# Hybrid decoder block: first norm's scales moved into the token transfer, the first roundings and warm-ups rearranged, the residual transposes moved behind the query tiles

## The chip, the cores and the metric

The kernel runs on one core of one Trainium2 chip. The metric is the device time of one execution in microseconds (us), lower is better. Engines are named as in the profile: PE is TensorE's matmuls and PEld its weight loads, DVE is VectorE, ACT is ScalarE, POOL is GpSimd, SP is SyncE, which here only issues transfers.

## What is computed

One layer of a decoder block on 256 tokens of width 1024, float32. Cut to what matters here:

```python
def reference(x, ...):
    xn = rmsnorm(x, norm1_g)                    # per token: x * rsqrt(mean(x*x) + EPS) * g
    x = x + hybrid_mixer(xn, ...)               # conv branch + dilated attention, both gated, then W_out
    hn = rmsnorm(x, norm2_g)
    return x + peer(hn, ...)                    # product keys: query projection, scores, top 16, experts

def hybrid_mixer(xn, w_in, ...):
    proj = xn @ w_in                            # GLU input, q, k, v, two gates: 5376 columns
    ...
def peer(xn, w_q, sub_keys, u_tab, v_tab):
    q = (xn @ w_q)                              # 8 heads x 2 halves of 128: 16 query tiles
    s = einsum(q, sub_keys)                     # scores against 2 x 128 keys a head
    ...                                         # top 16 of 16 x 16 candidates, softmax -> gate
    h = einsum(u_tab[e], xn)                    # computed densely: all 128 U tiles
    return einsum(gelu(h) * gate, v_tab[e])     # and all 128 V tiles
```

## The kernel before, in words

**Layout.** The tokens lie transposed in `resid`, [128, 8, 256]: feature in the partition, eight blocks `k` of 128 features, 256 tokens as columns. All weights come as tiles of [128, 1024] (512 KB), 76 for the front (`front`: 8 GLU, 12 q and k, 6 v, 16 gates, 6 attention, 4 convolution and 8 mixer output tiles, then 16 query tiles, numbers 60 to 75), then 128 of U and 128 of V. Every tile goes through a ring of four slots: SP loads it into `raw` (L387), ScalarE rounds it to `hi` (`split_hi`, L335), VectorE or GpSimd makes the rest `lo = raw - hi` (`split_lo`, L354), and TensorE forms three products for each block k, hi x high part, hi x low part, lo x high part of the vector: 24 matmuls of 256 columns for one tile (`product`, L1218). `by_dve` says which engine makes a tile's lower half: VectorE for tiles 0 and 1 and for every fourth tile (3, 7, ... 75), GpSimd for the others. `load` of tile n waits for the lower half of tile n - 4, `split_hi` of tile n for TensorE's end of tile n - 4, TensorE's tile n for its lower half. Each engine works its queue in the order in which the code writes it.

**The start.** TensorE first runs `WARM_UP` matmuls on a tile of ones (L1233; two passes each in the profile). SP issues the tokens in two transfers of four blocks (L382, `x_in`), then tiles 0 to 2, the parameters, tile 3. ScalarE issues a transfer of its own for norm 1's scales (L475, `gain_in`). Norm 1 isn't applied before the first GLU tiles: these take `x * g` instead, and the factor of each token is applied to the result. The high part `xg_hi` of the first `XG_ACT` = 5 blocks is made by ScalarE (L481), that of the last three by VectorE (L748); the low part `xg_lo` of all eight by VectorE (`x_lo`, L738). The first two tiles' high products (L1242) run first, then their lower products (L1249), then the same for tile 2, then the sums of squares of the tokens (L1265, `ssq1`), for which ScalarE squares (L485, L488) and VectorE adds in pairs (L756, L760). Then come ScalarE's root (L493), VectorE's reciprocal (L764) and the normalisation for all later tiles.

**The middle.** After the GLU tiles, VectorE runs 31 taps of the depthwise convolution for four blocks (L794, L798) between its other work. Attention, convolution and mixer tiles follow; the mixer's output is added into `resid` (L975).

**The query tiles.** In the loop over u of the 16 query tiles (60 + u), ScalarE casts tile 63 + u and, for u from 4 to 11, the high part of block u - 4 of norm 2 (L469). VectorE makes a lower half where `by_dve` says so, then the normalisation of block u - 4 (`normalise`, L727 and L719), then the scaled copy of the query tile (`times_rs2`, L982). TensorE runs tiles 0 and 1, the sums `ssq2`, then tile 2, and behind tile 2 the 16 transposes of `resid` into banks 0 to 3 (L1440, `y_began`), where the V products add to them at the end. After tile 15 come 64 score matmuls (L1451), whose results ScalarE copies out (L639), and then the loop over the U tiles. GpSimd, when it has made all its lower halves up to tile 78, waits for `y_began`, writes `iota_nk` (L456) over memory that `resid` held, and goes on with the U tiles' lower halves, the next of which waits for ScalarE's cast of tile 79.

Of the kernel before, what the change touches and what calls it, by code (L numbers as in the profile page):

```python
# [11 lines left out]
ALU = mybir.AluOpType  # L12
# [3 lines left out]
P = 128  # L16
D = 1024
T = 256
# [36 lines left out]
WARM_UP = 27  # L55
# [17 lines left out]
XG_ACT = 5  # L73
# [92 lines left out]
def hybrid_block(nc, x_t, front, cols, rel_bias, onehot, sub_keys, u_tiles, v_tiles, out):  # L166
    bias_row = nc.dram_tensor("bias_row", (HEADS, BW), F32, kind="Internal").ap()
    toeplitz = nc.dram_tensor("toeplitz", (HEADS, P * BW), F32, kind="Internal").ap()
    with ExitStack() as ctx:
# [19 lines left out]
        def tmp(name, shape, dt=F32):  # L189
            return sb(name, shape, dt, inner)  # L190
# [28 lines left out]
        resid = tmp("resid", [P, KB, T])  # L219
# [50 lines left out]
        gain_in = sem("gain_in")  # L270
        square_run, acc_pairs = sem("square_run"), sem("acc_pairs")
        hi_ready = sem("hi_ready")
# [107 lines left out]
        def _(sp):  # L380
            for r in range(2):
                sp.dma_start(resid[:, 4 * r:4 * r + 4, :], x_t[:, 4 * r:4 * r + 4, :]).then_inc(x_in[r], 16)  # L382
# [82 lines left out]
        def _(a):  # L465
# [9 lines left out]
            a.dma_start(prm[:, C_N1:C_N1 + KB], cols[:, C_N1:C_N1 + KB]).then_inc(gain_in, 16)  # L475
            a.preload_act_table(ACT.Sqrt)
            a.wait_ge(gain_in, 16)
            for k in range(XG_ACT):
                if k % 4 == 0:
                    a.wait_ge(x_in[k // 4], 16)  # L480
                a.activation(xg_hi[:, k, :], resid[:, k, :], ACT.Copy, scale=prm[:, C_N1 + k:C_N1 + k + 1])\  # L481
                 .then_inc(xhi, 1)
            split_hi(a, 0, 0, 0)
# [218 lines left out]
        def _(dve):  # L702
# [12 lines left out]
            def normalise(gain, round_, ks):  # L715
# [7 lines left out]
                for k in ks:  # L723
                    if round_ == 0:
# [3 lines left out]
                                             scalar=prm[:, gain + k:gain + k + 1],  # L728
# [5 lines left out]
            def x_lo(k):  # L734

                dve.wait_ge(xhi, k + 1)
                i, gain = k % KB, (C_N1, C_N2)[k // KB] + k % KB
                dve.scalar_tensor_tensor(out=xg_lo[:, i, :], in0=resid[:, i, :], scalar=prm[:, gain:gain + 1],  # L738
# [3 lines left out]
            dve.wait_ge(gain_in, 16)  # L742
            for k in range(XG_ACT):
                if k % 4 == 0:
                    dve.wait_ge(x_in[k // 4], 16)
                x_lo(k)
            for k in range(XG_ACT, KB):
                dve.tensor_scalar(xg_hi[:, k, :], resid[:, k, :], prm[:, C_N1 + k:C_N1 + k + 1], None, ALU.mult)\  # L748
                   .then_inc(xhi, 1)
                x_lo(k)  # L750
# [121 lines left out]
            for n in range(T_ATT):  # L872
                if n > 0:
                    lo_of(n + LEAD)
                if n in NORM_AT:
                    normalise(C_N1, 0, NORM_AT[n])
# [108 lines left out]
            for u in range(HALVES):  # L985
# [6 lines left out]
                if 4 <= u < 4 + KB:  # L992
                    normalise(C_N2, 1, (u - 4,))
# [204 lines left out]
        def _(pe):  # L1198
# [37 lines left out]
            def high_products(b, n):  # L1236

                pe.wait_ge(hi_ready, n + 1)
                for k in range(KB):
                    pe.wait_ge(xlo, k + 1)  # L1240
# [192 lines left out]
            for u in range(2, HALVES):  # L1433
                step(full(T_WQ + u, ("wq", u), xg_hi, xg_lo))
                if u == 2:

# [191 lines left out]
```

## Time and profile before

| | us |
|---|---|
| median of 3 runs | 996.57 (996.49 to 997.5) |
| the profiled execution | 997.07 |
| its span in the profile | 995.2 |
| outside the span | 1.87 |
| TensorE busy | 989.8 |
| VectorE busy | 774.9 |
| ScalarE busy | 506.8 |
| GpSimd busy | 465.3 |

Times in the profile count from the start of the span. An engine's busy time is the union of its instructions' times; a matmul row's time runs to its modelled end, which overlaps the next one's start, so how fast products follow each other is read from where rows start, or from the chain of waits, whose pieces join without a gap. The chain goes back from the last instruction, at each step to what released it.

### The profile page before, as it was taken

How to read it: one execution, taken by the hardware profiler on the slowest of the kernel's cores; microseconds unless marked ns; L12 is line 12 of the kernel's file. 1: busy time of each engine (PE TensorE's matmuls, PEld its weight loads, DVE VectorE, ACT ScalarE, POOL GpSimd, SP SyncE). 2: the span in 40 equal slices, each digit the busy share in tenths (PEclk: the TensorE clock that was granted, in tenths of full speed). 3: DMA queues.
4: the chain of work that ended last, by engine and by line, in shares of the span. 5: the costliest groups of instructions: out<-in, count | busy, mean ns of one | idle time of the engine just before them, and what ended most of it. 6: DMA issues, size and time to landing. Idle time of an engine off the chain costs nothing.

```text
span 995.2 us, 21854 instructions
## 1 busy us (share of the span) xinstructions
PE 989.8 (99%) x7822; PEld 917.0 (92%) x7822; DVE 774.9 (78%) x1304; ACT 506.8 (51%) x789; POOL 465.3 (47%) x198
## 2 busy tenths in 40 slices
PE   9999999999999999999999999999999999999998
PEld 9998999999999999999999999888888888888887
DVE  5999784868899996097777777988888876776764
ACT  6663877544555544544444444444444445554443
POOL 3664366656689999874444444100000004344442
PEclk9999999999999999999999999999999999999999
DMA  6684445654455565555555555555554555556562
GB/s 242 211 308 150 149 148 162 212 201 149 150 197 200 171 211 188 191 176 184 177 180 174 182 172 169 185 175 170 177 180 171 182 174 190 190 189 195 186 203 90
DMA packets 52619, 181.95 MB, mean 183 GB/s; under 512 B 5943, under 2 KB 9155, under 8 KB 52452
## 3 DMA queue, kind: packets, MB, share of 16 engines
q1 hardware_dynamic: 52292, 181.16, 54.4%
q8 instruction: 25, 0.41, 0.2%
q10 hardware_dynamic: 288, 0.27, 0.1%
q14 instruction: 14, 0.11, 0.0%
HBM read 180.33 MB, written 3.43 MB: 185 GB/s over the span
## 4 chain that ended last, share of the span: by engine, by line
PE 93%; DVE 5%; ACT 1%; issue 0%; POOL 0%; ACTq 0%; DVEq 0%; POOLq 0%
PE bank L1218 50%; PE bank L1527 35%; DVE bank L798 3%; PE bank L1476 3%; PE bank L1319 1%; PE bank L1233 1%; PE bank L1451 1%; DVE lo L354 1%; PE bank L1242 1%; PE bank L1553 1%; PE bank L1335 1%; ACT hi L335 0%; PE bank L1358 0%; PE bank L1346 0%; PE bank L1249 0%
## 5 line engine op out<-in xcount | busy, mean ns | idle before, releaser
L354 POOL TENSOR_TENSOR lo<-raw,hi 128x1024 fp32r<-128x1024 f32 x184 | 462.4, 2527 | 515.9 <-ACT hi L335 515.4
L335 ACT CAST hi<-raw 128x1024 fp32r<-128x1024 f32 x332 | 348.0, 1049 | 218.0 <-PE bank L1527 186.3
L1218 PE MATMUL bank<-norm_space,hi 128*128 128x256 f32 x2624 | 452.4, 278 | 0.2 <-POOL lo L354 0.2
L1218 PEld LDWEIGHTS bank<-norm_space,hi 128*128 128x128 f32 x2624 | 396.2, 188 | 1.8 <-issue 1.2
L1218 PE MATMUL bank<-norm_space,lo 128*128 128x256 f32 x1312 | 362.8, 277 | 0.0
L1527 PE MATMUL bank<-hi,norm_space 128*128 128x512 f32 x1008 | 273.8, 391 | 0.0
L1218 PEld LDWEIGHTS bank<-norm_space,lo 128*128 128x128 f32 x1312 | 246.4, 188 | 0.0
L1527 PEld LDWEIGHTS bank<-hi,norm_space 128*128 128x128 f32 x1008 | 188.0, 188 | 38.5
L354 DVE TENSOR_TENSOR lo<-raw,hi 128x1024 fp32r<-128x1024 f32 x148 | 189.2, 1279 | 27.4 <-ACT hi L335 27.3
L1527 PE MATMUL bank<-lo,norm_space 128*128 128x512 f32 x504 | 155.5, 390 | 0.0
L1145 DVE TENSOR_TENSOR norm_space<-act,norm_space 128x256 fp32r<-128x256 f32 x128 | 111.7, 876 | 48.8 <-ACT norm_space L665 48.8
L645 ACT ACTIVATE act<-bank 128x256 f32 (+1 forms) x128 | 49.2, 384 | 187.8 <-PE bank L1218 187.8
L1527 PEld LDWEIGHTS bank<-lo,norm_space 128*128 128x128 f32 x504 | 94.6, 188 | 19.7
L1218 PE MATMUL bank<-rounded_space,hi 128*128 128x256 f32 x496 | 87.0, 280 | 0.0
L1138 DVE SCALAR_TENSOR_TENSOR act<-bank,act 128x512 f32 (+1 forms) x64 | 41.4, 686 | 51.7 <-PE bank L1476 51.7
L1126 DVE TENSOR_TENSOR ohB<-eqB,parts 128x1024 f16<-128x1024 f16 x64 | 81.4, 1272 | 0.0
L1218 PEld LDWEIGHTS bank<-rounded_space,hi 128*128 128x128 f32 x496 | 75.4, 188 | 0.9 <-issue 0.6
L1218 PE MATMUL bank<-rounded_space,lo 128*128 128x256 f32 x248 | 69.1, 278 | 0.0
L665 ACT CAST norm_space<-act 128x256 fp32r (+1 forms) x128 | 51.4, 402 | 0.1
L1218 PEld LDWEIGHTS bank<-rounded_space,lo 128*128 128x128 f32 x248 | 47.0, 190 | 0.0
L798 DVE SCALAR_TENSOR_TENSOR bank<-u_pad,prm,bank 128x256 f32<-128x256 f32 x116 | 46.3, 481 | 0.0
L1122 DVE TENSOR_TENSOR ohA<-iota_nk,keys 128x1024 f16<-128x1024 f16 x64 | 46.1, 720 | 0.0
(183 smaller groups left out, 651.5 us busy)
## 6 DMA issues: line engine op xcount, KB each, us to landing
raw<-u_tiles SPq DMA_DIRECT2D x128, 512.0 KB, 3.3
raw<-v_tiles SPq DMA_DIRECT2D x128, 512.0 KB, 3.3
raw<-front SPq DMA_DIRECT2D x76, 512.0 KB, 3.8
toeplitz<-bias_row SPq DMA_DIRECT2D x6, 384.0 KB, 7.5
bias<-toeplitz SPq DMA_DIRECT2D x12, 128.0 KB, 3.5
resid<-x_t SPq DMA_DIRECT2D x2, 512.0 KB, 4.7
qk<-sub_keys SPq DMA_DIRECT2D x1, 1024.0 KB, 8.0
y<-act SPq DMA_DIRECT2D x3, 256.0 KB, 2.0
```

What stands on the lines that cost most here:

```text
L335: act_e.copy(hi[:, s, :], raw[:, s, :]).then_inc(hi_ready, 1)
L354: eng.tensor_tensor(lo[:, s, :], raw[:, s, :], hi[:, s, :].bitcast(F32), ALU.subtract)\
L645: a.activation(act[:, it * 4 + (base_i + j), :], bank[4 + j % 2][:, 0:T], ACT.Gelu).then_inc(gelu_done, 1)
L665: a.copy(act_hi[:, (base_i + j) % RING, :], act[:, it * 4 + (base_i + j), :]).then_inc(a_hi, 1)
L798: dve.scalar_tensor_tensor(out=acc[:, b, :] if w == TAPS - 1 else part_sum, in0=src, scalar=wt, in1=part_sum, op0=ALU.mult, op1=ALU.add).t ...
L1122: dve.tensor_tensor(ohA[:, g % 2], every_pair(iota_nk[:, :, :], NK), at(keys[:, 0, t], NK), ALU.is_equal).then_inc(spread, 1)
L1126: dve.tensor_tensor(ohB[:, g % 2].rearrange("p a i n b -> p (a i) n b"), eqB[:, :, :, :].unsqueeze(2).broadcast_to([P, TOK // PAIR, 2, HAL ...
L1138: dve.scalar_tensor_tensor(out=av, in0=gv, scalar=1.0 / GATE_SCALE, in1=av, op0=ALU.mult, op1=ALU.mult)\
L1145: dve.tensor_tensor(act_lo[:, s, :], act[:, it * 4 + (base_i + j), :], act_hi[:, s, :].bitcast(F32), ALU.subtract).then_inc(a_lo, 1)
L1218: ins = pe.matmul(dst, w_[:, s, u * P:(u + 1) * P], x_[:, k, :], start=first and i == 0 and p_ == 0, stop=last and i == n - 1 and p_ == 2)
L1476: ins = pe.matmul(bank[6 + g][:, q * HALF:(q + 1) * HALF], ohA[:, g, q // PAIR, :, q % PAIR], ohB[:, g, q // PAIR, i, :, q % PAIR], start= ...
L1527: ins = pe.matmul(bank[2 * c + half][:, :], a_[:, j, c * P:(c + 1) * P], v_[:, j, half * 512:(half + 1) * 512], start=False, stop=False, s ...
```

## The change

Norm 1's scales stand in the first eight columns of the same input rows as the tokens, and one SBUF tensor `x_space` holds both; the first of the two transfers is 8 columns longer, and ScalarE's own transfer with its semaphore is gone. ScalarE makes all eight `xg_hi`; VectorE makes only low parts. Tile 0 is cast in two operations of 512 columns, the first with a semaphore of its own (`hi_first`), which TensorE's first four blocks wait for. There are 21 warm-ups for 27. The residual transposes stand after the last query tile, ahead of the scores. The core of the diff:

```diff
@@ -52,7 +52,7 @@
 PICK_TILE = 60
 HALF = NK // 2
 GATE_SCALE = 2.0 ** 15
-WARM_UP = 27
+WARM_UP = 21
 G_SHARED = N_FRONT + HALF + LEAD
 TOK = 8
 PAIR = 2
@@ -70,7 +70,7 @@
 LNSUM_AT, LNVAR_AT = 33, 37
 RS2_AT = 2
 
-XG_ACT = 5
+X_CHUNKS = ((0, 4), (4, 8))
 NORM_AT = {2: (0, 1), 3: (2, 3), 4: (4, 5), 5: (6, 7)}
 TAPS_IN = {8: 1, 9: 2, 10: 2, 11: 2, 12: 1, 13: 2, 14: 2, 15: 2, 16: 1, 17: 2, 18: 2, 19: 2, 20: 1, 21: 1, 22: 2,
            23: 1, 24: 1, 25: 1, 26: 1, 27: 1, 30: 1}
@@ -216,7 +216,8 @@
         gains = tmp("gains", [P, 1])
         stat = tmp("stat", [P, 16, TC * HEADS])
 
-        resid = tmp("resid", [P, KB, T])
+        x_space = tmp("x_space", [P, KB + KB * T])
+        norm1_g, resid = x_space[:, 0:KB], x_space[:, KB:].rearrange("p (k t) -> p k t", t=T)
         inner.close()
         act = sb("act", [P, NK, T])
         iota_nk = sb("iota_nk", [P, NK, PAIR], F16)
@@ -267,9 +268,8 @@
-        gain_in = sem("gain_in")
-        hi_ready = sem("hi_ready")
+        hi_ready, hi_first = sem("hi_ready"), sem("hi_first")
@@ -378,8 +378,9 @@
 
         @block.sync
         def _(sp):
-            for r in range(2):
-                sp.dma_start(resid[:, 4 * r:4 * r + 4, :], x_t[:, 4 * r:4 * r + 4, :]).then_inc(x_in[r], 16)
+            for r, (first, end) in enumerate(X_CHUNKS):
+                columns = slice(KB + first * T if r else 0, KB + end * T)
+                sp.dma_start(x_space[:, columns], x_t[:, columns]).then_inc(x_in[r], 16)
 
             def load(src, base, it, j):
                 if not (isinstance(it, int) and base + 4 * it + j < RING):
@@ -472,15 +473,14 @@
                 job_done(a, ("bias", h))
                 a.copy(p3[0:HEADS, h, :], bank[BANK_OF[("bias", h)]][0:HEADS, 0:BW]).then_inc(act_evac, 1)
 
-            a.dma_start(prm[:, C_N1:C_N1 + KB], cols[:, C_N1:C_N1 + KB]).then_inc(gain_in, 16)
             a.preload_act_table(ACT.Sqrt)
-            a.wait_ge(gain_in, 16)
-            for k in range(XG_ACT):
-                if k % 4 == 0:
-                    a.wait_ge(x_in[k // 4], 16)
-                a.activation(xg_hi[:, k, :], resid[:, k, :], ACT.Copy, scale=prm[:, C_N1 + k:C_N1 + k + 1])\
-                 .then_inc(xhi, 1)
-            split_hi(a, 0, 0, 0)
+            for r, (first, end) in enumerate(X_CHUNKS):
+                a.wait_ge(x_in[r], 16)
+                for k in range(first, end):
+                    a.activation(xg_hi[:, k, :], resid[:, k, :], ACT.Copy, scale=norm1_g[:, k:k + 1]).then_inc(xhi, 1)
+            wait_raw(a, 0, 0, 0)
+            a.copy(hi[:, 0, 0:D // 2], raw[:, 0, 0:D // 2]).then_inc(hi_first, 1)
+            a.copy(hi[:, 0, D // 2:D], raw[:, 0, D // 2:D]).then_inc(hi_ready, 1)
             split_hi(a, 1, 0, 0)
             a.activation(sq[:, 0:4, :], resid[:, 0:4, :], ACT.Square).then_inc(squared, 1)
             split_hi(a, 2, 0, 0)
...
@@ -734,20 +734,16 @@
             def x_lo(k):
 
                 dve.wait_ge(xhi, k + 1)
-                i, gain = k % KB, (C_N1, C_N2)[k // KB] + k % KB
-                dve.scalar_tensor_tensor(out=xg_lo[:, i, :], in0=resid[:, i, :], scalar=prm[:, gain:gain + 1],
+                i = k % KB
+                gain = prm[:, C_N2 + i:C_N2 + i + 1] if k >= KB else norm1_g[:, i:i + 1]
+                dve.scalar_tensor_tensor(out=xg_lo[:, i, :], in0=resid[:, i, :], scalar=gain,
                                          in1=xg_hi[:, i, :].bitcast(F32), op0=ALU.mult, op1=ALU.subtract)\
                    .then_inc(xlo, 1)
 
-            dve.wait_ge(gain_in, 16)
-            for k in range(XG_ACT):
-                if k % 4 == 0:
-                    dve.wait_ge(x_in[k // 4], 16)
-                x_lo(k)
-            for k in range(XG_ACT, KB):
-                dve.tensor_scalar(xg_hi[:, k, :], resid[:, k, :], prm[:, C_N1 + k:C_N1 + k + 1], None, ALU.mult)\
-                   .then_inc(xhi, 1)
-                x_lo(k)
+            for r, (first, end) in enumerate(X_CHUNKS):
+                dve.wait_ge(x_in[r], 16)
+                for k in range(first, end):
+                    x_lo(k)
             lo_of(0)
             lo_of(1)
             for i in range(2):
...
@@ -1235,8 +1231,11 @@
 
             def high_products(b, n):
 
-                pe.wait_ge(hi_ready, n + 1)
                 for k in range(KB):
+                    if n == 0 and k < KB // 2:
+                        pe.wait_ge(hi_first, 1)
+                    else:
+                        pe.wait_ge(hi_ready, n + 1)
                     pe.wait_ge(xlo, k + 1)
                     for x_ in (xg_hi, xg_lo):
                         pe.matmul(b[:, 0:T], hi[:, n, k * P:(k + 1) * P], x_[:, k, :],
@@ -1432,16 +1431,14 @@
             step(pe.matmul(b[:, 0:T], ones[:, :], sq[:, KB - 1, :], start=False, stop=True))
             for u in range(2, HALVES):
                 step(full(T_WQ + u, ("wq", u), xg_hi, xg_lo))
-                if u == 2:
-
-                    freed(pe, ("mix", KB - 1))
-                    for c in range(TC):
-                        for k in range(KB):
-                            ins = pe.matmul(bank[2 * c + k // 4][:, (k % 4) * P:(k % 4 + 1) * P],
-                                            resid[:, k, c * P:(c + 1) * P], ident[:, :], is_transpose=True,
-                                            start=k % 4 == 0, stop=False, skip_group_check=True)
-                    ins.then_inc(y_began, 1)
             assert done[0] == FRONT_STEPS
+            freed(pe, ("mix", KB - 1))
+            for c in range(TC):
+                for k in range(KB):
+                    ins = pe.matmul(bank[2 * c + k // 4][:, (k % 4) * P:(k % 4 + 1) * P],
+                                    resid[:, k, c * P:(c + 1) * P], ident[:, :], is_transpose=True,
+                                    start=k % 4 == 0, stop=False, skip_group_check=True)
+            ins.then_inc(y_began, 1)
             pe.wait_ge(sk_in, 16)
             for j in range(N_SC):
                 b = start(("sc", j))
@@ -1608,7 +1605,8 @@
         np.tile(a["q_norm_g"][0], 2)[:, None], np.tile(a["k_norm_g"][0], 2)[:, None],
     ], axis=1)
     arrays = {
-        "x_t": a["x"][0].T.reshape(KB, P, T).transpose(1, 0, 2),
+        "x_t": np.concatenate([col(a["norm1_g"][0]),
+                               a["x"][0].T.reshape(KB, P, T).transpose(1, 0, 2).reshape(P, KB * T)], axis=1),
         "front": front,
         "cols": cols,
         "rel_bias": a["rel_bias"],
```

## Rows read from the trace of the kernel before

**Rows 1.** The page, busy time by engine.

```profile
PE 989.8 (99%) x7822; PEld 917.0 (92%) x7822; DVE 774.9 (78%) x1304; ACT 506.8 (51%) x789; POOL 465.3 (47%) x198
```

**Rows 2.** The chain of waits in time: start us, us, engine, tile, line, count.

```profile
1.17 8.82 PE bank L1233 x54
9.98 3.64 PE bank L1242 x32
...
18.16 0.86 PE bank L1265 x4
...
43.25 9.40 DVE bank L798 x24
...
83.29 0.71 PE bank L1306 x4
...
113.97 8.68 PE bank L1218 x72
...
153.06 57.34 PE bank L1218 x504
...
211.26 2.76 PE bank L1218 x24
214.02 1.75 PE bank L1440 x16
215.77 36.75 PE bank L1218 x312
...
259.66 163.29 PE bank L1218 x1440
```

**Rows 3.** TensorE's timeline: start us, us, engine, line, operation.

```profile
9.74 3.89 PE L1242 MATMUL bank<-rounded_space,hi 128*128 128x256 f32 x32
```

**Rows 4.** Stretches for L1233: length, busy (count), PE clock, DMA share, GB/s.

```profile
2.00:6.00 4.00, 4.00 (x20) 4.00 (x20) 1.00 0.90 310
6.00:8.00 2.00, 2.00 (x18) 2.00 (x17) 1.00 1.00 408
```

**Rows 5.** ScalarE's timeline at the start, in brackets its idle time before.

```profile
5.14 2.11 ACT L481 ACTIVATE rounded_space<-resid,prm 128x256 fp32r<-128x256 f32 x5 [2.65 <-DMA prm<-cols]
7.86 1.05 ACT L335 CAST hi<-raw 128x1024 fp32r<-128x1024 f32 x1 [0.61 <-DMA raw<-front]
9.12 1.05 ACT L335 CAST hi<-raw 128x1024 fp32r<-128x1024 f32 x1 [0.21 <-DMA raw<-front]
...
11.98 1.11 ACT L488 ACTIVATE bank<-resid 128x512 f32<-128x512 f32 x2
```

**Rows 6.** The tokens' two transfers (tile x_t): first and last issue, landing times.

```profile
L382 SPq DMA_DIRECT2D resid<-x_t x2: 400/408/417, 0.8 to 1.2; - x2
...
DMA to landing us min/median/max: 4.2/4.7/5.2
```

**Rows 7.** VectorE's timeline at the start.

```profile
5.79 2.07 DVE L738 SCALAR_TENSOR_TENSOR rounded_space<-resid,prm,rounded_space 128x256 fp32r<-128x256 f32 x5 [5.79 <-ACT rounded_space L481]
...
15.77 0.68 DVE L760 TENSOR_TENSOR sq<-sq,bank 128x512 f32<-128x512 f32 x1
```

**Rows 8.** TensorE's waits, 70 to 90 us: us in total, times, longest.

```profile
PE bank L1306 <- DVE rk_parts L900: 0.8, 1, 0.8
```

**Rows 9.** VectorE's timeline, lower half of tile 75.

```profile
245.33 3.41 DVE L354 TENSOR_TENSOR lo<-raw,hi 128x1024 fp32r<-128x1024 f32 x1
```

**Rows 10.** GpSimd's timeline, lower halves of tile 76 and of 79 and 80.

```profile
245.25 2.41 POOL L354 TENSOR_TENSOR lo<-raw,hi 128x1024 fp32r<-128x1024 f32 x1 [0.46 <-ACT hi L335]
...
262.73 4.76 POOL L354 TENSOR_TENSOR lo<-raw,hi 128x1024 fp32r<-128x1024 f32 x2 [7.92 <-ACT hi L335]
```

**Rows 11.** ScalarE's timeline, casts of tiles 67 and 76.

```profile
218.69 1.05 ACT L335 CAST hi<-raw 128x1024 fp32r<-128x1024 f32 x1 [3.25 <-PE bank L1218]
...
244.13 1.05 ACT L335 CAST hi<-raw 128x1024 fp32r<-128x1024 f32 x1 [0.21 <-PE bank L1218]
```

**Rows 12.** The page's costliest groups: count, busy us, mean ns, idle before.

```profile
L354 DVE TENSOR_TENSOR lo<-raw,hi 128x1024 fp32r<-128x1024 f32 x148 | 189.2, 1279 | 27.4 <-ACT hi L335 27.3
```

More of the change, by code:

```diff
@@ L727, in normalise @@
                     dve.scalar_tensor_tensor(out=whole(k, round_), in0=resid[:, k, :],
-                                             scalar=prm[:, gain + k:gain + k + 1],
+                                             scalar=gain[:, k:k + 1],
                                              in1=inv, op0=ALU.mult, op1=ALU.mult).then_inc(normed, 1)
@@ L875, in _ @@
                 if n in NORM_AT:
-                    normalise(C_N1, 0, NORM_AT[n])
+                    normalise(norm1_g, 0, NORM_AT[n])
                 if n < T_QK:
@@ L992, in _ @@
                 if 4 <= u < 4 + KB:
-                    normalise(C_N2, 1, (u - 4,))
+                    normalise(prm[:, C_N2:C_N2 + KB], 1, (u - 4,))
                 if u >= RS2_AT:
```

## The prediction

> **What bounds the kernel now.** I read the page's busy times first, then the chain of waits in order of time, then each engine's timeline where the change touches it. TensorE is busy 989.8 of 995.2 us [rows 1]: a saving counts only if it lets TensorE start earlier, closes a hole in its stream or makes its products follow each other faster. Work taken off VectorE or ScalarE counts for nothing by itself. The chain [rows 2] shows where TensorE is the bound. It runs the warm-ups from 1.17, the first products from 9.98 and the sums of squares of norm 1 (L1265) at 18.16. Between about 35 and 83 us the chain is on ScalarE and VectorE (the convolution taps, L798), and from 83.29 on it is on TensorE nearly always.
>
> The same rows, divided by their counts, show something that no idle time shows. From 153.06, 504 products take 57.34 us: 113.8 ns each. From 215.77, the 312 products of query tiles 3 to 15 take 36.75 us: 117.8 ns each. From 259.66, 1440 products of the same shape take 163.29 us: 113.4 ns each [rows 2]. So L1218 has two paces, some 4.4 ns apart. The slow one begins right behind the 16 residual transposes (L1440, at 214.02) and is over at 259.66, behind the score products. Tile 2, just before the transposes, took 2.76 us for 24: 115.0 ns each. The slow pace isn't bound to the transposes: 72 products from 113.97 take 120.6 ns each [rows 2]. I don't know its cause; in these rows it changes only where other work interrupts the stream.
>
> **Part one, the start.** Today the first product starts at 9.74 [rows 3], when the warm-ups end. Their rate shows the clock: 20 passes (as counted) in the 4 us from 2 to 6, 18 in the 2 us from 6 to 8 [rows 4]. The level goes from 1.2 to 2.4 GHz soon after 6, and the granted clock is written 1.00 throughout. Six warm-ups less are 12 of the 54 passes [rows 2], all at the fast end: 12 x 0.11 = 1.3 us, so TensorE is free at about 8.45. Nothing before that moment changes, so the clock should still have risen.
>
> Then it waits for data. ScalarE's rounding starts at 5.14 after a wait of 2.65 us for the scales' own transfer [rows 5]. The first half of the tokens landed at 0.8 + 4.2 = 5.0 and the second at 1.2 + 5.2 = 6.4 [rows 6]. With the scales in the same rows (32 bytes more on 4096) I take 5.0 for the start. Five pieces take 2.11 us, 0.42 each; eight take 3.4, to 8.4. Tile 0 has landed by then (its cast starts at 7.86 as soon as it lands). Its first half: two operations of 512 columns (L488) take 1.11, so I take 0.55, to 8.95 [rows 5]. The first product starts at about **9.0 instead of 9.74: 0.75 us**. Bounds: TensorE is never free before 8.45, so at most 1.3; if the half cast cost as much as a whole one, 1.05, the start would be 9.45 and the gain 0.3.
>
> What stands behind it. The second half is ready at about 9.45, and the products want it 8 passes after the start, at 9.9. Tile 1's cast, today 9.12 to 10.17, becomes 9.4 to 10.45; it is wanted at 9.0 + 1.8 = 10.8. VectorE's low parts, today from 5.79 in 2.07 us for five [rows 7], follow ScalarE at 0.42 and end at 9.0 instead of 10.2, because its three roundings (L748) are gone; its two lower tile halves then wait for the casts and end near 10.7 and 11.8, earlier than today. ScalarE's later work slips 0.2 to 0.3. The last sum of pairs (L760) starts today at 15.77 and takes 0.68 [rows 7]; it becomes 16.7, and TensorE wants it at 18.0 - 0.75 = 17.25. So the lead survives to the sums of squares, with half a microsecond to spare. From there ScalarE's root, VectorE's reciprocal and all normalisation hang on them, so the chain over VectorE moves by the same amount. TensorE's only wait on it later is 0.8 us for L900 [rows 8], and the waiting point moves too. I carry **0.75** through; bound from below 0, if that chain turns out to hang on transfers and not on the sums.
>
> **Part two, the transposes.** The same 16 run either way (1.75 us in the chain). What moves is their place. Without them query tiles 3 to 15 continue the stream of tile 2 at its pace. Thirteen tiles x 24 x (117.8 - 113.4) = **1.4 us**. They then stand between the last query tile and the scores, which need VectorE's evacuation of that tile anyway.
>
> The cover to check is the lower half of the tiles, since the tiles come 1.75 us earlier and then 0.1 us faster each. The one with least slack is tile 75, the last. Its lower half is made by VectorE at 245.33 and takes 3.41 us, to 248.74 [rows 9], because GpSimd's lower half of tile 76 runs from 245.25 to 247.66 [rows 10]; VectorE finishes 1.1 us after GpSimd. TensorE comes to tile 75 at 215.6 + 12 x 2.83 = 249.5: 0.8 us of slack. After the change it comes at 213.9 + 12 x 2.72 = 246.5, 3.0 us earlier. The chain to that half goes back over ScalarE and VectorE to the cast of tile 67 at 218.69, which waited for TensorE (3.25 us) [rows 11]; that point moves with tile 63's end, from 218.4 to 216.6, 1.85 us. At 244.13 there is another wait of 0.21 us for TensorE, which vanishes. So the half is ready at about 248.74 - 1.85 - 0.2 = 246.7, and 246.9 with a collision at the start, where VectorE's half of tile 67 now meets GpSimd's of tile 66. TensorE **waits about 0.6 us** with the semaphore's latency (bounds 0 and 1.0). Net of part two: **0.8 us**.
>
> The Trainium skill, page "SBUF — State Buffer", section "SBUF: two separate sides", says that VectorE with two SBUF inputs and GpSimd share a port pair under an exclusive lock, and that the later one is blocked for the whole instruction. The trace agrees: 3.41 us where L354 on VectorE takes 1.28 on average [rows 12]. By that rule the half can't escape by being asked for earlier; if the rule didn't hold here, the 0.6 us would be nothing.
>
> GpSimd's iota waits for the transposes and is now behind the last query tile; after it GpSimd sits idle for 7.92 us [rows 10], so this costs nothing. No transfer is issued in either place. ScalarE's queue loses the issue of the scales' transfer, and SP's keeps its order. The one new wait (hi_first) holds back all of TensorE, but the old one on the whole tile stood in its place.
>
> **Sum.** 0.75 + 0.8 = 1.55 us. The profiled execution took 997.07, of which 995.2 is the span; the median shown is 996.57, 0.5 below. From the median: 996.57 - 1.55 = **995.0**. The span of a profile would be about 993.6.
>
> **Rivals.**
> (a) *More comes through.* TensorE doesn't wait at tile 75, or the tokens land earlier without 128 small packets beside them: 1.2 + 1.4 = 2.1 to 2.6 us, time 994.2. For: both bounds allow it. Against: the collision on VectorE repeats in the same form. 0.16.
> (b) *A part is lost.* Either the lead of part one is swallowed between 35 and 83 us, or the query tiles run at the slow pace even without the transposes (then tile 75 doesn't wait either, and part two gives about 0.1), or another short stretch falls to the slow pace (the 504 products from 153 us: +2.0). Time 995.8 to 997.0. For: the slow row at 113.97, which has no transposes before it. 0.23.
> (c) *Slower: the U tiles fall to the slow pace.* In the row at 259.66 they start behind the score products and keep 113.4 ns for 1440 products. If the restart behind the moved transposes and scores settles at 117.8, it costs 1440 x 4.4 ns = 6.3 us: 996.57 - 1.55 + 6.3 = 1001.3. It decides the sign once about 350 products, 15 tiles, run slow. For: nothing in the rows says why a restart goes one way, and this one is the longest uninterrupted stretch. Against: the scores, their order and the wait behind them are unchanged. 0.08.
> (d) *The start doesn't do what it says*: TensorE idles and its clock falls back to 1.2 GHz. The idle time would be 0.5 us; the 0.8 us before L1306 [rows 8] didn't do it: 4 products in 0.71 us follow [rows 2]. Price: some 2 us. 0.03.
> The forecast itself (1.1 to 2.0 us) 0.50.
>
> **Range.** 993.8 to 997.8. It leaves out (c) and half of (d). A measurement can tell about 0.2% here, 2.0 us. Faster by more: most of (a) and the tail of the forecast, 0.25. Slower by more: (c), 0.09. Within: 0.66.
>
> **What would show it.** First product (L1242) at 9.0 with a hole of 0.5 us behind 42 warm-up passes; L1265 at 17.4; L1306 earlier by 0.75; the 13 query tiles in 35.4 us plus one wait before the last; 16 transposes directly before L1451; 1440 products in 163.3 us. Wrong would be: no shift at L1306, 117.8 ns in the query tiles, or 169 us for the U tiles.

## The result

| | before | after |
|---|---|---|
| median, us (15 executions each) | 997.14 | 1002.56 |
| lowest to highest | 996.36 to 997.5 | 997.5 to 1002.91 |
| profiled execution, us | 997.07 | 1002.6 |
| its span | 995.2 | 1000.8 |

The ratio is 1.0052, with a 95% interval of 1.0046 to 1.0059: slower, where 995.0 and "within 0.2%" were forecast. 14 of the 15 executions of the changed kernel lie near 1002.5 and one at 997.5; there is nothing between. Two executions beside the experiments, one of the kernel before (1012.7 us) and one with a matmul over the ones (1414.58 us), ran at a granted clock of 0.949 and 0.654 for the 1.00 of the others, and are left out of every count. The rival that came true is (c), which was given a chance of 0.08.

The changed kernel's page has TensorE no less busy than [rows 1], and ScalarE and GpSimd as before:

```profile
span 1000.8 us, 21850 instructions
PE 994.4 (99%) x7810; PEld 920.9 (92%) x7810; DVE 767.6 (77%) x1301; ACT 507.9 (51%) x793; POOL 466.2 (47%) x198
```

The chain of the changed kernel in time, as [rows 2]: start us, us, engine and line, count. A line number of the kernel after is 1 to 4 lower than that of before from L900 on (L1214 was L1218, the products; L1241 was L1242; L1264 was L1265; L1305 was L1306; L1438 was L1440, the transposes; L1448 was L1451, the scores; L978 was L982).

```profile
1.17 6.35 PE bank L1229 x42
7.52 1.12 issue
8.63 4.01 PE bank L1241 x32
...
17.35 0.88 PE bank L1264 x4
...
82.48 0.71 PE bank L1305 x4
...
113.16 8.68 PE bank L1214 x72
...
211.65 1.76 DVE rs L985
213.42 0.02 issue
213.44 0.43 DVE prob L978
213.88 0.04 issue
213.92 32.93 PE bank L1214 x288
246.87 3.07 PE bank L1214 x24
249.94 1.75 PE bank L1438 x16
251.69 7.15 PE bank L1448 x64
258.84 169.67 PE bank L1214 x1440
428.50 0.44 PE bank L1488 x4
```

What to see, from top to bottom. The norm's sums (L1264) start 0.81 us earlier than in [rows 2], at 17.35 for 18.16, and L1305 also 0.81 earlier. At 213.92 TensorE comes out of a wait for VectorE that [rows 2] doesn't have. Twelve query tiles then run at 32.93 / 288 = 114.3 ns a product with a wait of 0.2 us in it, the fast pace. The U tiles start at 258.84 instead of 259.66, so 0.82 us is in hand there. And then the same 1440 products take 169.67 us instead of 163.29: 117.8 ns each for 113.4, 6.38 us. That is the whole of the loss: 6.38 - 0.82 = 5.56, and the spans differ by 5.6. What follows the U stage takes equally long.

Nothing waits in those 169.67 us. The view of TensorE's waits has four for the whole span (us in total, times, longest):

```profile
PE bank L1229 <- POOL ones L435: 1.2, 1, 1.2
PE bank L1241 <- issue: 1.1, 1, 1.1
PE bank L1214 <- DVE prob L978: 0.7, 1, 0.7
PE bank L1214 <- POOL lo L354: 0.2, 1, 0.2
```

The last row names GpSimd; the lower half that ended last before the restart at 246.87 is VectorE's, of tile 75, at 246.72 (its row stands further down).

So the question for the experiments: why does a stage whose instructions, data and inputs are unchanged run 3.9% slower?

### The profile page after: what moved, and what is told of

Same layout as the page of the kernel before. It is cut to its first block, busy times and chain, and to the rows that moved or that the text cites. A ratio compares the mean times of both kernels' runs of the same rounds, so it can differ in the third digit from the quotient of the medians.

```text
span 1000.8 us, 21850 instructions
## 1 busy us (share of the span) xinstructions
PE 994.4 (99%) x7810; PEld 920.9 (92%) x7810; DVE 767.6 (77%) x1301; ACT 507.9 (51%) x793; POOL 466.2 (47%) x198
## 4 chain that ended last, share of the span: by engine, by line
PE 96%; ACT 2%; DVE 1%; issue 1%; POOL 0%; ACTq 0%; DVEq 0%; POOLq 0%
PE bank L1214 51%; PE bank L1524 34%; PE bank L1473 3%; PE bank L1318 2%; PE bank L1448 1%; ACT hi L335 1%; PE bank L1229 1%; PE bank L1241 1%; PE bank L1550 1%; PE bank L1334 1%; PE bank L1357 0%; DVE lo L354 0%; PE bank L1345 0%; PE bank L1248 0%; PE bank L1295 0%
## 5 line engine op out<-in xcount | busy, mean ns | idle before, releaser
L1214 PE MATMUL bank<-norm_space,hi 128*128 128x256 f32 x2624 | 459.6, 280 | 0.2 <-POOL lo L354 0.2
L1214 PEld LDWEIGHTS bank<-norm_space,hi 128*128 128x128 f32 x2624 | 398.8, 189 | 1.8 <-issue 1.2
L1214 PE MATMUL bank<-norm_space,lo 128*128 128x256 f32 x1312 | 365.5, 279 | 0.0
L1214 PEld LDWEIGHTS bank<-norm_space,lo 128*128 128x128 f32 x1312 | 246.4, 188 | 0.0
L1214 PE MATMUL bank<-rounded_space,hi 128*128 128x256 f32 x496 | 85.9, 278 | 0.7 <-DVE prob L978 0.7
L1214 PEld LDWEIGHTS bank<-rounded_space,hi 128*128 128x128 f32 x496 | 74.9, 188 | 2.0 <-DVE prob L978 0.9
L1214 PE MATMUL bank<-rounded_space,lo 128*128 128x256 f32 x248 | 68.6, 277 | 0.0
L1214 PEld LDWEIGHTS bank<-rounded_space,lo 128*128 128x128 f32 x248 | 46.6, 188 | 0.0
```

The source lines that it names most:

```text
L1214: ins = pe.matmul(dst, w_[:, s, u * P:(u + 1) * P], x_[:, k, :], start=first and i == 0 and p_ == 0, stop=last and i == n - 1 and p_ == 2)
```

## The experiments

Three theories, named by letter in the expectations. **A**: how the first products of the stage fall in time, to some nanoseconds, draws one of two paces, and it is kept until something interrupts the stream. **B**: the kind of work just before (the transposes ahead of the scores) sets it. **C**: how the addresses of the columns (the normed tokens, `nrm`) stand to those of the weights (the slots `hi` and `lo`) decides which paces there are. The pace of a profile is its chain row divided by its count. In the text and the tables below a time near 996 is an execution with the U stage at 163.3 us, one near 1002.5 with it at 169.7, as each kernel's profiled execution shows for its own time; for executions without a profile that is inferred from the time.

### Which part brings it

**The start alone** (transposes left behind query tile 2, the rest as after), and **the transposes alone** (the kernel before with them behind the last query tile).

> Part one alone: scales with the tokens, ScalarE's eight roundings, tile 0 cast in halves, 21 warm-ups; the residual transposes stay behind query tile 2. Theory A (the pace of the 1440 U products, 113.4 or 117.8 ns each, is settled by nanoseconds at their one restart behind the scores, and anything that shifts the stream can tip it): U tiles 163.3 or 169.6 us, the time 996.3 or 1002.7 us, both possible within one kernel's executions. Theory B (the transposes standing directly before the scores make the U tiles slow): U tiles fast, 163.3 us, time 996.3. Under both the stream from 83 us on comes 0.8 us earlier, there is no wait of TensorE at query tile 3, and query tiles 3 to 15 take 36.75 us.

> The transposes moved alone, start as before. Theory A: U tiles 163.3 or 169.6 us. Theory B: slow, 169.6 us in every execution. Under both: TensorE waits 0.9 us before query tile 3, because its bank is freed by VectorE only after norm 2's reciprocal, which the transposes covered; the 13 query tiles save 1.2 us; without the U tiles' part the time would be 997.14 - 0.3 = 996.8, with it 1003.1.

The start alone gave 1002.43, 1002.49, 1002.76 and 1002.91. The transposes alone gave 996.13 to 997.13 in seven executions and 1004.39 to 1004.8 in three; the profiled one is of the slow three, which lie above 1002.5: the start's lead is missing, and in the profile the query tiles are slow too. The chain, first of the start alone, then of the transposes alone:

```profile
213.35 1.75 PE bank L1439 x16
215.09 36.75 PE bank L1214 x312
251.84 7.14 PE bank L1450 x64
258.99 169.67 PE bank L1214 x1440
```

```profile
214.79 37.01 PE bank L1218 x312
251.80 1.75 PE bank L1439 x16
253.55 7.15 PE bank L1449 x64
260.69 169.66 PE bank L1218 x1440
```

The first has the scores alone ahead of the U tiles, as the kernel before has, and it is slow; the second has the changed order and was fast in 7 of 10. Theory B falls in its simple form. The second also takes away a step of part two: there are no transposes ahead of these 312 query products, and they still go at 118 ns. The profiles of the two runs that follow say the same with 37.02 us for these 312, where the changed kernel's own took 36.00: of five profiles with the transposes moved and query tile 3 on its old bank, three have the slow pace in the query tiles.

### Timing alone

Three edits of the changed kernel or of the one before that move no data and change only what stands just ahead of the U stage, or when it comes.

**A matmul of 128 columns between scores and U tiles**, and **27 warm-ups again**:

```diff
+            freed(pe, ("sc", 4))
+            for _ in range(1):
+                pe.matmul(bank[7][:, 0:P], ident[:, :], ident[:, :], start=True, stop=True)
```
```diff
-WARM_UP = 21
+WARM_UP = 27
```

> The changed kernel with one more matmul (identity times identity, 128 columns, 0.2 us, into a bank that nobody needs) between the scores and the first U tile. Its result is read by nobody. Theory A: the restart falls at another moment, so the U tiles may run fast: if so 1002.56 - 6.3 + 0.2 = 996.5. Theory B: still slow, 1002.8.

> The changed kernel with 27 warm-ups again. The first product then starts behind the warm-ups, near 9.7 instead of 8.63, so everything up to the U tiles comes some 0.8 us later. Theory A: the U tiles go either way, 169.6 (time 1003.3) or 163.3 (997.0). Theory B: slow, 1003.3.

The first gave 997.36 once and 1002.66 to 1003.06 four times; the second 997.62 once and 1003.38 to 1003.91 four times. In both the profiled execution is the fast one:

```profile
259.75 0.29 PE bank L1457 x2
260.03 163.22 PE bank L1214 x1440
```

```profile
251.33 1.75 PE bank L1438 x16
253.08 7.15 PE bank L1448 x64
260.22 163.29 PE bank L1214 x1440
```

So the changed order of work can run fast. The pace is one of two, and both come up with one and the same kernel.

**The waits before U tile 0 parted** in the kernel before, and the same in the kernel after. TensorE waits for ScalarE's copies of the last two score banks before it starts tile 0; here tile 0 waits for one of them, tile 1 for the other. The start of the first U product stands 103 ns behind that of the last score product in the trace of before, and 31 ns in this one.

```diff
-            for job in JOBS[-4:]:
-                if BANK_OF[job] < 6:
-                    freed(pe, job)
+            freed(pe, ("sc", 5))
...
+                if j == 1:
+                    freed(pe, ("sc", 6))
```

> The kernel before, but the wait for ScalarE's copies of the scores in front of the U tiles is parted: U tile 0 waits for the copy of score job 5 alone (its own bank), tile 1 for that of job 6. In the kernel before, the first weight load of the U tiles starts 182 ns behind the last of the scores, not 112: it is released by the copy of job 6. Theory A1 (the pace is a lottery where TensorE restarts on another engine's release; where it restarts without a wait the outcome is fixed by the program): the gap shrinks to 112 ns and every execution is alike, all with U tiles in 163.3 us (time 997.0) or all in 169.6 (1003.4). Theory A2 (any restart is a lottery, wait or not): executions of both kinds.

> The same edit in the changed kernel. A1: the U restart no longer depends on ScalarE, so it goes the same way as in the kernel before with the same edit, in every execution: 996.2 (fast) or 1002.5 (slow), with 1.4 us of scatter left from the restart at query tile 3, where TensorE still waits for VectorE. A2: both kinds, as now.

The kernel before, fast in all 79 executions on record here (15 in the result, 64 beside the runs), gave 1002.54, 1003.07, 1003.26 and 1003.73 with this edit: slow in four of four. Its chain:

```profile
216.12 36.75 PE bank L1218 x312
252.87 7.14 PE bank L1451 x64
260.01 169.60 PE bank L1218 x1440
```

The kernel after stayed slow (1002.39 to 1003.39). Here nothing of the change is present, only 72 ns are gone ahead of the stage, and the whole loss appears. The starts of the first products differ by as little: from the third on the steps are 117, 117, 123, 118, 113 ns in before, and 118, 118, 118, 117 ns in this one. This is the strongest case for theory A, as far as it says that a small step is enough. The size of the gap is not what decides: in the kernel after the first U product stands 104 ns behind the last score product, for 103 in before, the next steps are 193, 117 and 118 ns for 194, 117 and 117, and its profile is slow; the profile with 27 warm-ups has the gap and the first steps of before to the nanosecond, and is fast. The slow and the fast stream part at the step that comes next, 118 ns for 123. What makes them part isn't shown.

### The wait at query tile 3

The changed kernel's wait of 0.7 us is for the bank of query tile 3, which holds tile 0's result until VectorE has copied it (L978), and that copy needs the reciprocal of norm 2 (L985, 211.65 to 213.42 in the chain above). Before, the transposes filled the time. **Tile 3 on bank 1**, which is free by then, and **the same with the waits parted**:

```diff
+BANK_OF[("wq", 3)] = 1
...
             freed(pe, ("mix", KB - 1))
+            freed(pe, ("wq", 3))
```

> The changed kernel with query tile 3 in bank 1, which is free there, instead of bank 6, which VectorE frees only after norm 2's reciprocal. The wait of 0.9 us before query tile 3 goes, query tiles 2 to 15 run in one stream at 113.3 ns until tile 75's lower half, where the wait grows from 0.2 to about 1 us, so the gain is small: scores 0 to 0.3 us earlier than in the changed kernel. The U tiles: A1 and A2 both leave them open, 163.3 or 169.6 us, since their restart still waits for ScalarE. Time 996 or 1002.3.

> Both edits. A1: as for the changed kernel with the parted wait, all executions alike in the U tiles, and the query tiles fast in all of them: 996.0 or 1002.3, scatter under 0.7 us. A2: both kinds of execution.

Bank 1 gave 995.69 and 995.8, then 1001.74 to 1002.33 eight times; with the waits parted 995.48 and 995.59, then 1001.66 to 1002.23 eight times. The wait at tile 3 is gone, and the U tiles start at 258.07 in the first, 0.77 us earlier than in the kernel after. Both its levels lie below those of the kernel after (one execution at 997.5; 1002.56), by 1.8 and some 0.5 us. All nine profiles below with tile 3 on bank 1 and the tokens at 8 elements or more, the slots in their old place, have query tiles 2 to 14 at the fast pace. It doesn't cure the pace, and a restart with no wait before it isn't always slow or always fast: the part of theory A that said so fell.

**Four matmuls of 64 float16 columns**, or **one of 256 columns over the ones**, ahead of the U tiles of the last kernel:

> The changed kernel with query tile 3 in bank 1 and the parted wait (all named bank1_split), and four float16 matmuls of 64 columns (of the identity's bits, read by nobody) between the scores and the U tiles. In every profile so far the products that follow the gates' float16 matmuls run fast but for one stretch of two tiles. Theory A2 (the pace is settled in the first few products behind an interruption, by how the stream before it ended): fast in most executions, 163.3 us for the U tiles, time 995.6 + 0.2 = 995.8. If what ended the stream doesn't matter: slow in 8 of 10 executions as in bank1_split, 1002.1.

> bank1_split with one float32 matmul of 256 columns with the tile of ones as weights between the scores and the U tiles, the kind that stands before query tile 2 (L1432 in the kernel before), behind which the products have run fast in each profile. Theory A2: fast in most executions, 995.9 (0.3 us dearer). But the same kind stands before a slow stretch at 123 us, so if the odds aren't tied to the kind of matmul: 1002.2 in most.

Four small ones: 995.83 to 996.2 in four executions, 1002.05 to 1002.56 in six. One large: 995.6 to 996.18 in five, 1002.45 to 1002.64 in four. Neither is certain, and whether they shift the odds isn't shown: with so few executions 2 of 10 and 5 of 9 can't be told apart firmly, and these two ran on another chip than the kernel that they are compared with.

### Is it kept until an interruption?

**A matmul of one column at the head of each pass** (four tiles) of the loop over U tiles 4 to 59, in the kernel with bank 1 and parted waits:

```diff
+            freed(pe, ("sc", 4))
             with pe.Fori(1, PICK_TILE // RING) as it:
+                pe.matmul(bank[7][:, 0:1], ident[:, :], ident[:, 0:1], start=True, stop=True)
```

> bank1_split with one float32 matmul of a single column at the head of each of the 14 loop passes over U tiles 4 to 59: 14 more interruptions, each some 0.1 us. Theory A2: the pace is drawn anew at each, so that of the 15 stretches of four tiles some are fast and some slow in each profile; with half of them fast the U tiles take 163.3 + 14 x 0.1 + 3.2 = 168 us, time 1000.2, between the two kinds. If the pace were a state that only the long history sets: all slow, 1003.4, or all fast, 997.

1001.82 to 1002.25. The chain, each row four tiles of 24 products:

```profile
257.79 11.31 PE bank L1215 x96
269.22 11.01 PE bank L1215 x96
280.34 11.42 PE bank L1215 x96
291.88 11.01 PE bank L1215 x96
303.00 11.42 PE bank L1215 x96
314.54 11.01 PE bank L1215 x96
```

After the first row, 114.7 and 119.0 ns a product in strict turn, for as long as the interruptions last. A row's time includes the step past the interruption; the products between go at 113.3 and 117.8 ns. Each interruption redraws the pace, though here not at random: the turns alternate. The passes of 96 U products in the later loops are parted by 32 other matmuls, and go at 10.98 us each in either kernel: there every restart comes out fast. Why there and not here isn't shown.

### The addresses

**The normed tokens 32 bytes lower**, all else as with bank 1 and parted waits:

```diff
-        nrm = norm_space[:, SHIFT:].rearrange(...)
+        nrm = norm_space[:, 0:KB * 2 * T].rearrange(...)
```

> bank1_split with norm 2's high and low parts (the U tiles' moving operand) 32 bytes lower in SBUF. Theory C (the slow pace is a collision of the weight reads and the moving reads in memory, which depends on how their addresses stand to each other): the U tiles take a pace other than 113.3 and 117.8 ns, or only one of them. If the addresses don't matter: the same two paces, mostly slow, 1001.9.

1014.77 to 1015.78: U stage 170.89 us in the chain, with the query tiles (39.58 us for 336 products) and the later U loops slow too. A change of 8 elements in a start address, with the same instructions, costs 13 us beyond the slow pace: 1.3 of them in this stage, 3.0 ahead of it, the rest in the later U loops, whose passes take 11.48 us for 10.98. So I moved it the other way, with the slots where they are (`iota`, 16 columns, gives its place to the larger buffer and stands behind the slots). These three and the next have query tile 3 on bank 1, but the waits before U tile 0 as in the kernel after:

> The same with the array begun 12 elements (48 bytes) in. Theory C: a place that isn't a multiple of 32 bytes; if each row read crosses one more border of some width, every product is slower, 1010 us and more; if the place within 32 bytes is nothing to the engine, as begun at 8: 995.6 and 1002 in a mix.

> The same with the array begun 16 elements (64 bytes) in. Theory C: if what counts is the distance in steps of 32 bytes, this place stands as far from the weights' (96 bytes modulo 128) as 0 stands from 32 modulo 64, and I expect 1002 us or slower; if only the place at 0 is bad, 995.6 and 1002 in a mix.

> The changed kernel with query tile 3 on bank 1, and the array of the normed tokens begun 24 elements (96 bytes) into its buffer instead of 8 (32 bytes); the weight slots stay where they are. Theory C (the pace of a run of products hangs on how the addresses of the columns stand to those of the weights): another place, another mix; begun at 0 it was 170.97 us for the U stage, so a place on the other side may let it hold 163.3 us in every execution, 995.5 us in all. If the place at 0 was bad by itself and every other place is alike, the two times of before return: 995.6 and 1002 in about one to four.

And the control, with the enlarged buffer but the tokens at 8 elements as ever:

> Control for the three places: the same enlarged buffer and moved little array, but the normed tokens begin at 8 elements as ever. Theory C: two times in a mix, near 995.6 and near 1002 us, as with query tile 3 on bank 1. If the layout edit itself cost the 17 to 24 us of those runs, this one is at 1012 or slower, and theory C isn't shown by them.

| tokens begin at element | executions, us | U stage in the chain |
|---|---|---|
| 0 | 1014.77 to 1015.78 | 170.89 |
| 8, control | 995.82; 1001.82 to 1002.19 four times | 163.28 (the fast one) |
| 12 | 1015.18 to 1015.66 | 171.66 |
| 16 | 1012.19 to 1012.56 | 170.46 |
| 24 | 1019.04 to 1019.38 | 172.86 |

The place of before and after, 8, is the only one of the five at which a fast pace was seen in this stage at all. My hope that another would be fast in every execution fell.

Is it the tokens' own place, or their distance from the weights? **The slots moved up by 32 bytes, tokens at 8**, and **both moved by 32 bytes**:

```diff
+        slot_shift = sb("slot_shift", [P, 8])
         hi = sb("hi", [P, RING, D], F32R)
```

> The rounded weight slots moved up by 8 elements (32 bytes), the normed tokens left at 8. If it is the distance, this is like moving the tokens down by 32 bytes (begun at 0: U stage 170.97 us, 1014.8 us in all): the U stage at 170 us or more in every execution. If it is the columns' place alone: U stage 163.3 or 169.7 us, about 995.6 or 1002 us.

> The normed tokens at 16 elements, and the rounded weight slots moved up by 8 elements (32 bytes) too, so that the two stand to each other as in the kernel before. Alone, 16 elements gave 1012.4 us. If what counts is the distance, the U stage is back to 163.3 or 169.7 us (995.6 or 1002 us but for the stages that read the other arrays, whose distance is changed by this: up to 8 us more). If it is the place of the columns by itself, 170.5 us in the U stage and 1012 us in all.

The chains around the U stage, the slots alone first, then both:

```profile
262.44 169.03 PE bank L1216 x1440
...
826.79 184.87 PE bank L1527 x792
```

```profile
252.87 7.15 PE bank L1451 x64
260.02 163.29 PE bank L1216 x1440
...
447.94 11.39 PE bank L1216 x96
...
460.31 10.98 PE bank L1216 x96
...
814.59 184.87 PE bank L1527 x792
```

With the tokens alone at 16 the stage took 170.46; with the slots following them it is back at 163.29, the fast pace to the hundredth. With the slots alone moved it is 169.03. So neither place decides by itself: how the two arrays stand to each other counts. But the distance isn't the whole of it. Slots 32 bytes up and tokens 32 bytes down give the same distance, and the stage took 169.03 in one and 170.89 in the other, where 170 or more was expected. The V products are another case: the 792 of L1527, which don't read the normed tokens, take 179.64 us in the kernel before and with the tokens alone moved, and 184.87 in both kernels whose slots moved. That fits the distance and the slots' place alike, since the activations that they are multiplied with were never moved along:

```profile
822.21 179.64 PE bank L1526 x792
```

(This row is of the tokens at 16.) All in all the slots alone gave 1022.08 to 1022.24, and both together 1009.94 to 1010.12. The latter's span is 14.2 us above that of the control (1008.2 for 994.0): 9.4 of them are V products, 1.6 stand ahead of the U stage, and 3.2 are U products of the later loops, whose distance was kept. Their passes, 10.98 us each in the kernel before, alternate between 11.39 and 10.98 here, as in the run with the one-column matmuls. Theory C holds this far: a shift of one array against the other takes the fast pace away, and moving both brings it back. Which of the paces then comes up depends on the timing of theory A even so.

The kernel before was fast in all 79 executions, and the one with both arrays moved seems so in its four, which lie within 0.2 us of each other; no kernel here has the fast U stage every time and is faster than before. The one with bank 1 beats the kernel before by 1.0 us when it draws the fast pace (995.75 for 996.76, the median beside it) and loses 5.3 when it doesn't, which was eight times in ten.

## Why the prediction was wrong

- **The first product.** Forecast 9.0 and a hole of 0.5 us; measured 8.63, behind a hole of 1.12. ScalarE made its eight pieces in 3.30 us from 4.72, where I had 3.4 from 5.0. The warm-ups ended at 7.52, a microsecond before the 8.45 that I had worked out: this execution has 30 of their passes between 2 and 6 us, for 20 in [rows 4], so their rate rose earlier, from 11 passes in one 2 us stretch to 19 in the next (by these counts the levels of 1.2 and 2.4 GHz). In the run of the start alone, with the same 21 warm-ups, the stretch from 4 to 6 us has 11 and the warm-ups end at 8.56: the end of the warm-ups differs from one execution to the next. TensorE then waits for the data, and the granted clock stays at 1.00:

```profile
2.00:4.00 2.00, 2.00 (x11) 1.00 0.77 237
4.00:6.00 2.00, 2.00 (x19) 1.00 1.02 414
```

ScalarE's timeline at the start, with the eight pieces and the half cast that releases the first product:

```profile
4.72 3.30 ACT L480 ACTIVATE rounded_space<-x_space 128x256 fp32r<-128x256 f32 x8 [2.68 <-DMA x_space<-x_t]
7.93 0.60 ACT L482 CAST hi<-raw 128x512 fp32r<-128x512 f32 x1
```

- **Its lead.** Of 1.11 us at the first product 0.81 reached the sums of squares and L1305. I had 0.75 at both: right, by luck, since two errors cancel. What ate 0.3 us is the slow pace again: the 72 products before the sums took 8.56 us from start to start for 8.26 before (118.9 ns each for 114.7). The run with a matmul of 128 columns ahead of the U tiles, whose start is the same program, had them at the fast pace: its first product came 0.12 us later, at 8.75, and its sums 0.20 us earlier, at 17.15. The wait of [rows 8] is gone rather than moved.
- **The slow query tiles.** Forecast 35.4 us and one wait; measured 32.93 + 3.07 = 36.00 with a wait of 0.2 in it, against 36.75: 0.75 gained, of 0.8 forecast. The wait before the last tile was sized 0.6 and is 0.2: the lower half of tile 75 took 3.09 us and ended at 246.72, where I had 246.9 (VectorE's timeline):

```profile
243.63 3.09 DVE L354 TENSOR_TENSOR lo<-raw,hi 128x1024 fp32r<-128x1024 f32 x1
246.65 1.07 DVE L978 TENSOR_TENSOR prob<-bank,rs 128x256 f32<-128x256 f32 x3
```

But the reason given, that without the transposes the tiles continue the pace of tile 2, isn't what held: the last tile, interrupted by its 0.2 us, ran at 118 ns, and with the transposes moved alone all 312 products were slow. That the profiled execution had 12 tiles fast was a draw as well: with the same code at this place three of five profiles had none, and part two then gains nothing. With no wait at tile 3 (bank 1) they do continue the pace of tile 2.
- **The transposes' old place.** This step failed too, by a smaller amount. I costed the move at nothing but their own 1.75 us and looked for cover only at the lower halves. They had also covered norm 2's reciprocal: tile 3 needs the bank of tile 0, and waits 0.7 us for it. That is a term of the sum that I left out, and it eats the gain of the query tiles. At the start of the U stage the sum was 0.82 us in hand, not 1.55. The rule that I used at tile 75 (who frees it, when, and what covers that time) had to be put to every bank as well.
- **The U tiles.** This is the step that failed and made the time wrong: the sum carried the stage at 163.3 us, unchanged, and it took 169.67. I had seen the two paces, had priced the stage's fall at 6.3 us (measured 6.38, and (c) put the time at 1001.3 for the measured 1002.56) and had the mechanism in (c), but gave it 0.08 on the argument that "the scores, their order and the wait behind them are unchanged". The runs show in its place that the stage can come up slow after an edit anywhere ahead of it, near or far. An edit that leaves all of them in place, at the start of the kernel 240 us earlier, made the stage slow in four of four; so did 72 ns less before it. Twelve kernels here leave the distance of the operands alone and draw the pace once, the changed one among them: two were fast in half or more of their executions, ten slow in most. So any edit ahead of this stage had to be given the odds of a fresh draw. Nothing that stood ahead of the forecast gave those odds, and these counts, of 4 to 15 executions a kernel, give them only roughly.
- **What I had no row for**: that the kernel before draws the fast pace in 79 of 79. Its three times shown (996.49 to 997.5) are all fast; a kernel with two levels looks like one with a single level when it sits on one side.

**Still open.** What in the timing chooses (which of the reads meet, and where), why the kernel before is so steady, and whether a place exists at which only the fast pace is left. Five of the tokens' places were tried, and two of the slots'. That other engines or transfers bring the slow pace was not tested; against it speaks that the 1440 products keep their pace while VectorE goes from 39.5 us busy (340 to 380 us) to 9.4 in the kernel before and 1.5 in the kernel after (380 to 420 us). That the two operands' reads collide in SBUF is the obvious reading, but no run shows it directly.

## What to carry to other kernels

Where one stage of TensorE products holds a sixth of the time, divide each chain row by its count, compare the paces, and treat any edit ahead of that stage, however small, as able to flip it; take more than three executions of both kernels before believing a difference of this size. When a block of work is moved, list what every buffer it stood in front of was waiting for: it may have been cover for someone. And the start address of an operand is a parameter to sweep, against that of the other operand: here moving one array by 32 bytes cost 10 to 20 us beyond the slow pace, more than anything in the change.

## What the runs showed of the hardware

- A stream of float32r products of 256 columns, each with its own weights, ran at 113.4 or 117.8 ns a product with the granted clock at 1.00 in both, and didn't change by itself within 1440 products. At other distances of the operands it was 117.4 to 120.0 ns (169.03 and 172.86 us over 1440).
- An interruption by a matmul of one column was enough to change it (stretches of 11.42 and 11.01 us in turn).
- The Trainium skill, page "SBUF — State Buffer", section "SBUF: two separate sides", says that on the engine side TensorE never waits on anyone. These runs don't bear on other engines, but they show that TensorE's own pace does depend on where its two operands lie, by 6% (163.29 to 172.86 us), so "never waits" isn't enough to take a full pace for granted. The measurement decides.
- The Trainium skill, page "TensorE: Matmul & The Clock Gate", section "Back-to-back issue gap", gives for an isolated warm matmul about N / 2.4 + 2.5 ns, an estimate of 109 ns for 256 columns, and says that in a stream with weight loads the spacing is set by both. No stage of such products here went below 113.3 ns.
